# A streaming-encoder block on one core: waits for result stores split by pair, a root table loaded ahead, and one GpSimd split moved

## The reference

```
x = x + concat(rwkv7_group, sgu_group) @ w_out          # token mixing
x = x + mem_cross_attn(rmsnorm(x, norm2_g), mem, ...)   # 4 heads, 256 tokens
x = x + (silu(h @ w_gate) * (h @ w_up)) @ w_down        # h = rmsnorm(x, norm3_g)
return rmsnorm(x, norm_f_g)                             # final norm

def rmsnorm(x, g):
    return x * rsqrt(mean(x * x, axis=-1) + 1e-6) * g
```

## Time and profile before

| | |
|---|---|
| median of 3 runs | 3377.97 us (3366.06 to 3390.21) |
| profiled execution, its own time | 3370.79 us |
| span in its profile | 3368.9 us |
| TensorE busy | 3158.1 us (94%) |
| VectorE, ScalarE, GpSimd busy | 35%, 24%, 32% |
| TensorE clock granted, mean | 0.964 of full speed |
| half 1 of the tail | from about 2259 us to the end |

### The profile page before, as it was taken

One profiled execution on the slowest core, in us unless ns is written; L12 is line 12 of the kernel. 1 busy time (PEld: TensorE's weight loads), 2 busy tenths in 40 slices (PEclk: granted clock), 3 DMA queues, 4 the chain that ended last, 5 costly groups with the idle time before them and its releaser, 6 DMA issues.

```text
span 3368.9 us, 61985 instructions
## 1 busy us (share of the span) xinstructions
PE 3158.1 (94%) x26618; PEld 2634.8 (78%) x26618; DVE 1192.6 (35%) x1366; ACT 806.9 (24%) x1127; POOL 1079.4 (32%) x551
## 2 busy tenths in 40 slices
PE   6989999699989879999999999997999999999997
PEld 6768788588878768778888888876877888888885
DVE  4532552456665532323212221253232321122223
ACT  4102202234343321322311111121132321111111
POOL 6234222235353344034222222163404322222124
PEclk9989999789898989999999999998999999999998
DMA  5252222222222042011111111134201111111112
GB/s 176 100 178 88 86 88 100 70 70 56 73 58 70 24 161 69 25 32 50 50 44 50 50 50 44 50 106 132 74 19 38 50 44 50 50 50 44 50 50 75
DMA packets 142744, 230.89 MB, mean 69 GB/s; under 512 B 48480, under 2 KB 95712, under 8 KB 141792
## 3 DMA queue, kind: packets, MB, share of 16 engines
q1 hardware_dynamic: 142560, 228.13, 21.1%
HBM read 186.14 MB, written 41.94 MB: 68 GB/s over the span
## 4 chain that ended last, share of the span: by engine, by line
PE 72%; DVE 3%; issue 3%; POOL 1%; DMA 1%; ACT 1%; POOLq 0%; SPq 0%; DVEq 0%; ACTq 0%
PE ps L994 55%; PE ps L1223 2%; PE ps L1061 2%; PE ps L1225 2%; PE ps L1413 2%; PE ps L1434 2%; PE ps L1207 2%; PE ps L1177 1%; DVE tu L1572 1%; PE ps L1301 1%; DMA x<-in_xT 1%; POOL sq L480 1%; PE ps L1165 1%; PE ps L1133 1%; PE ps L1110 0%
## 5 line engine op out<-in xcount | busy, mean ns | idle before, releaser
L471 POOL TENSOR_TENSOR w_lo<-w_raw,w_hi 128x1024 fp32r<-128x1024 f32 x244 | 594.6, 2438 | 1864.3 <-ACT w_hi L659 1864.3
L994 PE MATMUL ps<-a_hi,w_hi 128*128 128x512 f32 x2368 | 930.1, 393 | 60.7 <-POOL w_lo L471 34.9
L994 PE MATMUL ps<-a_lo,w_hi 128*128 128x512 f32 x2368 | 927.0, 391 | 0.0
L994 PE MATMUL ps<-a_hi,w_lo 128*128 128x512 f32 x2368 | 733.4, 391 | 0.0
L659 ACT ACTIVATE w_hi<-w_raw 128x1024 fp32r<-128x1024 f32 x244 | 258.5, 1060 | 1796.2 <-PE ps L994 1615.3
L994 PEld LDWEIGHTS ps<-a_hi,w_hi 128*128 128x128 f32 x2368 | 448.4, 189 | 157.2 <-issue 63.8
L994 PEld LDWEIGHTS ps<-a_lo,w_hi 128*128 128x128 f32 x2368 | 448.1, 189 | 94.5 <-issue 1.2
L994 PEld LDWEIGHTS ps<-a_hi,w_lo 128*128 128x128 f32 x2368 | 447.7, 189 | 93.6
L994 PE MATMUL ps<-b_hi,w_hi 128*128 128x512 f32 x1216 | 475.8, 391 | 3.0 <-POOL w_lo L471 2.1
L994 PE MATMUL ps<-b_lo,w_hi 128*128 128x512 f32 x1216 | 473.8, 390 | 0.0
L994 PE MATMUL ps<-b_hi,w_lo 128*128 128x512 f32 x1216 | 374.8, 389 | 0.0
(11 more groups left out here) (205 smaller groups left out, 3373.1 us busy)
## 6 DMA issues: line engine op xcount, KB each, us to landing
w_raw<-in_weights SPq DMA_DIRECT2D x244, 512.0 KB, 3.6
zT<-z_out SPq DMA_DIRECT2D x44, 512.0 KB, 2.8
in_raw<-in_xT SPq DMA_DIRECT2D x8, 1024.0 KB, 8.4
suv<-zT SPq DMA_DIRECT2D x16, 512.0 KB, 5.0
y_in_raw<-yT SPq DMA_DIRECT2D x8, 1024.0 KB, 11.2
x<-in_xT SPq DMA_DIRECT2D x16, 512.0 KB, 5.9
outT<-normed SPq DMA_DIRECT2D x16, 512.0 KB, 3.4
zin<-zT SPq DMA_DIRECT2D x48, 128.0 KB, 2.3
```

What stands on the lines that cost most here:

```text
L471: pool.tensor_tensor(w_lo[:, u, :, :], w_raw[:, u, :, :], w_hi[:, u, :, :].bitcast(F32), ALU.subtract).then_inc(S["w_lo_done"], 1)
L994: mm = pe.matmul(slot(u)[:, nb, 0:w], wt[:, u, k, :], r[:, k, nb * w:(nb + 1) * w], start=(k == 0 and r is hi_in and wt is w_hi), stop=(k ...
```

## The change

Three edits.

**Store waits.** The stores count in four semaphores `fin_st0` to `fin_st3`, one for each pair of tiles, in place of one. On ScalarE the one wait ahead of the phase goes. The phase is written out (`residual_start`) in place of a loop, and in half 1 it waits for pair i - 1 of the stores between `hi(first_q + i, 0)` and the `split_x` behind it. The order of the other instructions is that of `residual_phase`.

**Root table.** After its last `hi` of each half, ScalarE takes a root of one column of constants into an unused column (`eps[:, 3:4]`), before it waits for the last additions to `x` and for the sums. The table of functions that holds the root is thereby needed earlier.

**GpSimd.** In the last phase of half 0 (n = 2), the split of B0,1 no longer follows GpSimd's square of tile 6 directly; it first waits until VectorE has signalled its square of tile 7. In the phases n = 0 and n = 1 the order stays, and in half 1 there is no such split.

```diff
-                  "prod_hi prod_lo s_ps ... o_ps o_hi o_lo fin fin_st "
+                  "prod_hi prod_lo s_ps ... o_ps o_hi o_lo fin fin_st0 fin_st1 fin_st2 fin_st3 "
...
-                                 normed[:, k:k + 1, :]).then_inc(S["fin_st"], 16)
+                                 normed[:, k:k + 1, :]).then_inc(S[f"fin_st{k // 2}"], 16)
                     if hf == 0:
                         load_residual(1, k // 2, k % 2)
-            sp.wait_ge(S["fin_st"], 16 * HALVES * KT)
+            for j in range(KT // 2):
+                sp.wait_ge(S[f"fin_st{j}"], 32 * HALVES)
...
                     squares(n, KT - 2)
-                    if q_next is not None:
+                    if n < 2:
                         split_job(q_next, 1)
-                    if n < 2:
                         squares(n, KT - 1)
+                    elif q_next is not None:
+                        pool.wait_ge(S["sumsq_done"], (done + n + 1) * KT)
+                        split_job(q_next, 1)
...
+                def stored(pair):
+                    if hf:
+                        act.wait_ge(S[f"fin_st{pair}"], 32 * hf)
+
+                def residual_start(first_q, dst, g):
+                    for i in range(1, PAIRS_OUT + 1):
+                        for u in range(2):
+                            hi(first_q + i, u)
+                            if u == 0:
+                                stored(i - 1)
+                            split_x(0, 2 * i - 2 + u, dst, g)
...
-                if hf:
-                    act.wait_ge(S["fin_st"], 16 * hf * KT)
-                residual_phase(0, q0, b_hi, G_ATT)
+                residual_start(q0, b_hi, G_ATT)
...
                 if hf == 0:
                     for u in range(2):
                         hi(q0 + PAIRS_TAIL, u)
+                act.wait_ge(S["zero_done"], 4)
+                act.activation(eps[:, 3:4], eps[:, 0:1], ACT.Sqrt).then_inc(S["root_ready"], 1)
                 act.wait_ge(S["job_out"], 2 * (q0 + PAIRS_TAIL))
                 split_rms(n0 + 2)
```

More of the change, by code:

```diff
@@ L208, in hybrid_block_kernel @@
         for n in ("const_in in0 in1 in2 in3 xr_in0 xr_in1 sqa_done ws_zero const_ready mixers_done w_raw0 w_raw1 w_hi_done w_lo_done job_done job_out act_in sq_done sumsq_done "
-                  "stat_ps stat_rt rstd_done z_ext_done z_dif_done z_out_done z_st0 z_st1 carry_done zero_done "
+                  "stat_ps stat_rt root_ready rstd_done z_ext_done z_dif_done z_out_done z_st0 z_st1 carry_done zero_done "
                   "kv_done v_tr v_trc kv_store kv_in x_new act_hi act_lo gate_s gate_a prod "
-                  "prod_hi prod_lo s_ps s_max s_neg s_exp s_rcp s_nrm p_tr p_ev o_ps o_hi o_lo fin fin_st "
+                  "prod_hi prod_lo s_ps s_max s_neg s_exp s_rcp s_nrm p_tr p_ev o_ps o_hi o_lo fin fin_st0 fin_st1 fin_st2 fin_st3 "
                   "rconst rconst_done zk0 zk1 zv0 zv1 zs0 zs1 lora_in gate_in gs_done ksq_done lwa_ps th_done sig_done cum_done wneg_done wx_done wend_done "
```

## The result

The changed kernel took 3340.09 us (median of 4, 3337.43 to 3342.22) beside 3372.01 us (median of 4, 3365.57 to 3390.21) for the kernel before: ratio 0.9896, 95% interval 0.9854 to 0.9939. Two later comparisons with more runs of the kernel before gave 0.9931 (0.9908 to 0.9955) and 0.9930 (0.9905 to 0.9954), so some 23.5 us. The forecast was 3354 us with a range of 3341 to 3367: the time lies just under the range.

The account below looks back on a forecast made before the run. TensorE, 94% busy, was taken as the bound, so only its pauses and low clock pay. B2,0 21.4 us earlier plus 1.3 at the end makes 22.7; from 3376.3 that gives 3354 us, range 3341 to 3367.

Parts of the forecast that it names:

- the level: Whole kernel before: starting time of 3376.3 us, the mean of four executions, from which the gain was subtracted.
- the same sum: Total gain of 22.7 us: 21.4 from B2,0 starting earlier on TensorE, plus 1.3 at the end.
- if stretches before 2259 us have moved: Sign against the prediction: parts ahead of the turn between halves, before 2259 us, shift in the profile.
- Edit 3: VectorE's square of tile 7 before the turn: 3.38 us falls to 1.23, moving TensorE's work up by 0.62 us.
- Edit 2: Before the root, in the turn and at the end: table load hidden, 1.3 us earlier each time.
- Edit 1: Turn on TensorE: B1,0's pause shrinks from 21.5 to 2.0 us, with removal of B0,0 behind normed the next limit.
- The price of the split inside `normed`: VectorE in the turn: GpSimd's split of B1,0 beside normed costs 0 to 2.15 us; 2.15 taken.
- The clock: TensorE after B1,0's remaining pause: clock falls to 0.50, costing 1.7 us, bounds 0 and 2.99.
- the first rival: At B1,0: no pause, or one too short for the clock; gain 25 to 26.4 us, 3351 us, chance 0.25.
- The weights of B2: B2,0 on TensorE: split ready at 2305.1, wanted at 2309.7, so covered by 4.6 us behind stores and reloads.
- Rivals 3 and 4: In the turn: pair signals no earlier than the backlog, 3364 us, chance 0.06; late program fetches, 3385 us, chance 0.02.
- rival 3: Turn, at B1,1: pair's signal no earlier than whole backlog, split 8 us late; gain about 12, 3364 us, chance 0.06.

Follow-up runs that it names:

- both_new: Changed kernel with VectorE's removal of B0,0 between fifth and sixth normed, and GpSimd alternating splits and squares in each half's last phase; 3337.17 us, ratio 0.9915.
- one_wait_behind: Changed kernel with one wait for all eight stores, placed behind hi of B1,0, instead of waits by pair; 3349.87 us, ratio 0.9969.
- early_removal: Changed kernel with VectorE's removal of B0,0 moved between the fifth and sixth normed; executed once, tail 2147.4 us.
- before_again: Kernel before, no edit, timed against itself; ratio 1.0013, tail 2171.4 us.
- after_again: Changed kernel run again with no edit, against the kernel before; median 3342.29 us, ratio 0.9931.

## Why the prediction was right and wrong

**The step that failed is the level.** "The mean of all four is 3376.3. I put the forecast from there." The kernel before has a level of 3364.6; only one run in ten of the 70 reaches 3376. From 3364.6 the same sum, 22.7 us, gives 3341.9, and 19 runs have a median of 3340.3. Of the 13.9 us between forecast and time, 11.7 are the level and 2.2 the sum and the scatter. The range was too narrow for the same reason: it took 10 us for the scatter of medians, while the start of the tail alone lies anywhere from 1180.21 to 1204.31 in twelve profiles. I had seen 24 us between three runs and had not asked which stretch they came from, which one profile can't tell. One of my signs that the prediction is wrong was "if stretches before 2259 us have moved". They did move, by 4 us down and 11 us up in two profiles of one and the same kernel, so the sign told nothing of the change.

**The sum held.** 22.7 us forecast; 24.3 between the medians of all runs; tails 2149.4 to 2150.0 in three profiles against 2171.4 and 2175.7, 23.8 between the means. The profiles alone don't bear it out to better than 2 us: over the stretches that the edits touch (b of half 0 to a of half 1, and b to c of half 1) the changed kernel is 24.7 us shorter than the first profile of before and 21.6 shorter than the second. With a ratio of 0.993 the gain is within 1%, which I had given 0.78; the first ratio, 0.9896, lay beyond it because its four runs of the kernel before stood high.

**Edit 3** as forecast: 1.23 us. TensorE gained a little more than the 0.62 us, since the second half of the sums follows the first after 1.72 us, where it was 2.50.

**Edit 2** as forecast, 1.3 us at the end: 1.28 to 1.29 in each kernel that has it. The load and a root of 0.20 us were hidden. The 2.66 us a switch of the Trainium skill (ScalarE: Activation LUTs, What ACT_TABLE_LOAD costs) would have shortened b to c by more than twice that. No drain shows here, nor does one where the load now stands 0.02 us behind a copy (2254.36 + 1.06 to 2255.44).

**Edit 1**: the removal of B0,0 behind `normed` was next, as forecast, with a pause of 1.88 us (2.0). The price of the split inside `normed`, taken from the square, was 2.13 (2.15), and holding the split back removed it. Worse by itself than in company: without edits 2 and 3 the pause was 3.16 us, and the clock fell.

**The clock** was the term of the sum that was mis-sized. I took 1.7 us for a fall behind the pause; behind 1.87 to 1.89 us it stayed up in all five profiles that have this pause, so the term is 0. With 0 in its place the sum is 24.4 us, and the medians of all runs say 24.3. I had gone by pauses of 1.59 us and a single one of 2.12 us; over ten profiles that same pause left the clock up in four. "Too short for the clock" is the condition of the first rival, which had a chance of 0.25 and is what happened. Its gain of 25 to 26.4 us was worked out for a pause of at most 1.5 us, though, and for a split that costs less.

**The weights of B2** were covered by less than I had worked out: `w_lo` was ready 0.8 us before B2,0 (split from 2299.93 to 2302.33, B2,0 at 2281.35 + 21.77 = 2303.12), not 4.6.

```profile
2298.79 1.06 ACT L662 ACTIVATE w_hi<-w_raw 128x1024 fp32r<-128x1024 f32 x1 [12.34 <-DMA w_raw<-in_weights]
2299.93 2.40 POOL L472 TENSOR_TENSOR w_lo<-w_raw,w_hi 128x1024 fp32r<-128x1024 f32 x1 [6.42 <-ACT w_hi L662]
```

1.7 us of the difference are the clock that didn't fall. As much again is the end of the backlog: I had ended it at 2302 by the earlier trace rows, but the last reload of the kernel before, issued at 2297.58, took 6.1 us to land, which is 2303.7. The weight tile itself came 1.2 us behind the last reload, where I had taken 1.5. It was covered, but only just, as 0.38 us in `both_new` shows.

**Rivals 3 and 4** did not come; rival 3's pause is what `one_wait_behind` makes by force, 8.47 us for 8 foretold.

## What to carry to other kernels

Put a wait in front of the instruction that needs it, not ahead of the phase: what stood behind it here was a weight copy that fed the bound engine. When the stall goes, look at what else the released engines start earlier, and against whom; a split moved by this edit stretched `normed` by 2.1 us, and an edit of order that took nothing away (`early_removal`) removed the pause that this left. And before a change of under 1% is forecast, find the stretch in which the runs scatter, and forecast from a level taken over many runs.

## What the runs showed of the hardware

**The pause and the clock.** TensorE's granted clock does not follow the length of a pause alone. Behind pauses of 1.59 us (48 of 48, in attention) and of 1.9 us (5 of 5) it stayed at 2.4 GHz, behind 3.16, 8.47 and 19.5 to 21.5 us it fell to 1.2. In between it did either: behind the 2.12 us pause ahead of the turn it fell in six profiles and not in four, behind attention's 2.78 us in 13 of 24. The same pause in two executions of the kernel before, at the same place of the work (windows: busy, granted clock, DMA), first `before`, then `before_again`:

```profile
1376.00:1400.00 24.00, 21.22 (x91) 0.93 0.07 23
```

```profile
1366.00:1390.00 24.00, 21.22 (x94) 1.00 0.08 23
```

Such a fall costs 1.7 us in attention (246.33 against 244.63 us for the stretch), 1.6 behind the 3.16 us and 3.0 behind the 21.50 us. What it costs depends on who else is nearly late. Ahead of the turn TensorE loses the same 1.7 us, but root c comes only 0.8 us later in the changed kernel (718.2 against 717.4) and 0.05 in the kernel before (720.38 against 720.33). For there, when the clock stays up, TensorE waits for GpSimd and VectorE instead, as in `before_again`:

```profile
2248.28 1.96 PE L1012 MATMUL ps<-sumsq,cst 128*128 128x512 f32 x4 [0.54 <-POOL sumsq L482]
2251.63 1.98 PE L1012 MATMUL ps<-sq,cst 128*128 128x512 f32 x4 [1.40 <-DVEq L1881]
```

**Where the executions differ.** The mixers, between 620 and 1130 us, take from 492 to 506 us from their first to their last step in twelve profiles. The granted clock over 620 to 1120 us, first in `early_removal` (492 us, tail starts at 1180.21), then in `after_again` (506 us, 1204.31):

```profile
620.00:1120.00 500.00, 442.11 (x13569) 0.93 0.25 64
```

```profile
620.00:1120.00 500.00, 446.51 (x13211) 0.89 0.25 64
```

TensorE is about nine tenths busy there, with many short pauses. Of the 24.1 us between the starts of these two tails, 14 lie in that stretch. The rest lies between the last step and the tail, a stretch that takes 66.7 to 69.0 us in eleven profiles and 78.3 in `after_again`. Over everything ahead of the tail the granted clock is 0.94 in `early_removal` and 0.91 in `after_again`; in all twelve profiles a lower clock there goes with a later tail, but not strictly. That the clock makes the whole scatter was not shown, nor which of the two is the cause: one step of `after_again` took 42 us where its others take 30 to 34, and no experiment held the clock.
